# Delta rule of a fused two-block trunk: key products without masks, beta folded into VectorE's join, and turned keys ahead of the second query job

## The reference, cut to what matters

```python
gc = jnp.cumsum(chunks(g), axis=-1)
decay = jnp.exp(jnp.where(lower, gc[..., :, None] - gc[..., None, :], -jnp.inf))
k_beta = k * beta[..., None]
m = jnp.where(idx[:, None] > idx[None, :],
              jnp.einsum('bhnid,bhnjd->bhnij', k_beta, k) * decay, 0.0)
a_mat = eye + m
t_inv = lax.linalg.triangular_solve(a_mat, eye, left_side=True, lower=True, unit_diagonal=True)
...
intra = jnp.einsum('bhnid,bhnjd->bhnij', q, k) * decay
# scan over the chunks:
v_new = u_i - w_i @ s
o_i = (q_i * jnp.exp(g_i)[..., None]) @ s + a_i @ v_new
```

## Time and profile before

| | |
|---|---|
| median of three runs | 1927.75 us (1924.67 to 1928.99) |
| the profiled execution | 1928.05 us, its span 1926.2 us |
| busy: PE, DVE, ACT, POOL | 1820.8, 522.7, 429.1, 74.6 us |
| mean granted TensorE clock | 0.971 |
| input projection, convolutions and block inverses | about 52 to 228 us of the span |
| scan and modulation | about 228 to 294 us |
| experts | about 360 to 866 us |
| second block | from about 866 us on |

### The profile page before, as it was taken

The page is one execution under the profiler, slowest core; times in us unless marked ns, Lnnn a source line. Parts: engine busy times, 40 slices in busy tenths (PEclk is TensorE's granted clock), DMA queues, the critical chain, the costliest instruction groups (busy, mean ns, idle before and its releaser), DMA issues.

```text
span 1926.2 us, 25090 instructions
## 1 busy us (share of the span) xinstructions
PE 1820.8 (95%) x10394; PEld 1413.9 (73%) x10394; DVE 522.7 (27%) x1141; ACT 429.1 (22%) x925; POOL 74.6 (4%) x72
## 2 busy tenths in 40 slices
PE   6969898799999999999899999999999999899997
PEld 3665676566566666678678888888886688788886
DVE  3779441410000000022421212221234312212113
ACT  2542221111011110121542221111224522211112
POOL 0251000100000000010000100000000000000000
PEclk9889798899999999999999999999999999899999
DMA  9101178199999999973313324444443132234420
GB/s 394 42 22 66 54 276 333 77 398 422 422 422 422 422 422 422 422 305 138 130 66 132 109 110 150 152 151 152 140 137 131 47 128 110 88 134 152 155 84 22
DMA packets 53645, 383.32 MB, mean 199 GB/s; under 512 B 6208, under 2 KB 6336, under 8 KB 7360
## 3 DMA queue, kind: packets, MB, share of 16 engines
q1 hardware_dynamic: 52272, 376.97, 50.1%
q10 hardware_dynamic: 1296, 5.24, 0.7%
HBM read 381.14 MB, written 1.05 MB: 198 GB/s over the span
## 4 chain that ended last, share of the span: by engine, by line
PE 88%; DVE 8%; ACT 3%; issue 1%; DMA 1%; ACTq 0%; DVEq 0%
PE ps L575 84%; DVE arena L1962 3%; PE ps L573 2%; DVE ring L1956 1%; PE ps L632 1%; DVE arena L1956 1%; DVE arena L1959 1%; DMA ipos<-in_pos 1%; ACT arena L1720 1%; DVE small L2429 0%; DVE ring L2095 0%; DVE arena L2327 0%; ACT L1455 0%; DVE arena L1970 0%; ACT arena L1828 0%
## 5 line engine op out<-in xcount | busy, mean ns | idle before, releaser
L575 PE MATMUL ps<-arena,ring 128*128 128x256 f32 (+2 forms) x3680 | 832.5, 387 | 9.1 <-DVE arena L1962 3.9
L575 PEld LDWEIGHTS ps<-arena,ring 128*128 128x128 f32 x3680 | 694.8, 192 | 135.7 <-issue 42.4
L575 PE MATMUL ps<-ring,arena 128*64 128x256 f32 (+4 forms) x3168 | 484.2, 418 | 0.0
L575 PEld LDWEIGHTS ps<-ring,arena 128*64 128x64 f32 (+1 forms) x3168 | 292.9, 148 | 175.2 <-issue 87.2
L575 PE MATMUL ps<-arena 128*128 128x128 f32 (+5 forms) x1256 | 202.2, 322 | 6.6 <-DVE rounds_i L2283 1.8
L575 PEld LDWEIGHTS ps<-arena 128*128 128x128 f32 (+3 forms) x1256 | 166.8, 189 | 37.5 <-issue 22.8
L1962 DVE SCALAR_TENSOR_TENSOR arena<-ps,par,arena 128x255 f32<-128x255 f32 (+1 forms) x178 | 74.3, 480 | 336.5 <-ACT arena L1932 335.6
L575 PE MATMUL ps<-ring 128*128 128x256 f32 (+2 forms) x896 | 116.1, 301 | 8.9 <-DVE ring L2113 7.8
L575 PEld LDWEIGHTS ps<-ring 128*128 128x128 f32 (+2 forms) x896 | 98.5, 163 | 22.8 <-issue 10.1
L1932 ACT ACTIVATE arena<-ps,par 128x256 f32<-128x256 f32 x88 | 42.4, 562 | 313.6 <-PE ps L575 313.6
L575 PE MATMUL ps<-arena,cst 128*128 128x256 f32 (+1 forms) x308 | 91.2, 442 | 11.7 <-ACT arena L1748 5.4
(11 more groups left out here) (176 smaller groups left out, 852.0 us busy)
## 6 DMA issues: line engine op xcount, KB each, us to landing
ring<-in_stream SPq DMA_DIRECT2D x358, 1024.0 KB, 10.4
arena<-in_xc ACTq DMA_DIRECT2D x1, 1024.0 KB, 5.3
xT<-in_xc ACTq DMA_DIRECT2D x1, 1024.0 KB, 8.8
arena<-in_mem ACTq DMA_DIRECT2D x1, 1024.0 KB, 4.9
out_y<-xT ACTq DMA_DIRECT2D x2, 512.0 KB, 2.7
ring<-in_dft ACTq DMA_DIRECT2D x1, 512.0 KB, 8.0
arena<-in_sguw ACTq DMA_DIRECT2D x2, 256.0 KB, 2.9
par<-in_par SPq DMA_DIRECT2D x1, 511.5 KB, 24.6
```

The costliest lines, as they stand in the source:

```text
L575: i = nc.tensor.matmul(out, lhsT, rhs, start=start, stop=stop, skip_group_check=skip)
```

## The change

The strict triangle goes (both as a constant and as products): what lies above the diagonal of `bX` is no longer zeroed. Beta goes from GpSimd into the join on VectorE, as a per-partition scalar of a three-operand instruction, one for each head. All four `gQ` now come from ScalarE's second ReLU, get their exp there, and one mask product each on GpSimd; beta enters those of c = 4 and 6 at the later join on VectorE. The order of three engines is changed: TensorE turns the keys ahead of the job of the third query quarter; VectorE scales the keys after `conv(0)` and runs `conv(1)` to `conv(3)` behind that; ScalarE takes the root ahead of the third quarter's evacuation, and has the exponentials of `gQ` behind its copies of the keys.

```diff
@@ gpsimd
-            def mask(c):
-                s, d = c // 2, c % 2
-                v = bX[:, 4 * c:4 * c + 4, :]
-                pool.wait_ge(exp_ok2, c + 1)
-                link(tt(v, v, over(beta[:, d, (s, s ^ 1)[d], :], full_h, 2)))
-                if s >= 2 and d == 0:
-                    tt(gQ[:, c - 4], v, over(C("cum0"), full_h)).then_inc(gq_ok, 1)
-                tt(v, v, over(C("strict"), full_h)).then_inc(xm_ok, 1)
-            for c in range(4):
-                mask(c)
             pool.wait_ge(l2_ps, 1)
             link(nc.gpsimd.memset(bZ, 0.0))
             nc.gpsimd.memset(flatZ[:, 0:BLK * BLK:BLK + 1], 1.0).then_inc(fill_ok, 1)
-            for c in range(4, 8):
-                mask(c)
             pool.wait_ge(free, SLOTS)
             nc.gpsimd.memset(bB, 0.0)
             nc.gpsimd.memset(bF, 0.0).then_inc(fill_ok, 1)
-            for k, c in enumerate((5, 7)):
+            for k in range(4):
                 pool.wait_ge(exp_ok2, 9 + k)
-                tt(gQ[:, c - 4], gQ[:, c - 4], over(C("cum1"), full_h)).then_inc(gq_ok, 1)
+                tt(gQ[:, k], gQ[:, k], over(C(f"cum{k % 2}"), full_h)).then_inc(gq_ok, 1)
@@ tensor
             for c in range(6, 8):
                 rows(c)
-            s = arrive()
-            job_a(s, 0, hX, T)
-
             pe.wait_ge(l2_sq, 1)
...
             for t in range(4):
                 turns(KB[t], lambda hd: kT[:, hd, tok(t)], tr_k)
+            s = arrive()
+            job_a(s, 0, hX, T)
+
             job_a(s, 1, hX, T)
@@ scalar, falls(c): one ReLU per head more for c = 4 and 6
-                        if s >= 2:
-                            i = A_(gQ[:, c - 4, hd, :], ..., bias=gc[:, d, t, hd:hd + 1])
+                    if s >= 2:
+                        i = A_(gQ[:, c - 4, hd, :], ..., bias=gc[:, d, t, hd:hd + 1])
@@ scalar
             for c in range(4, 8):
                 decays(bX[:, 4 * c:4 * c + 4, :], c)
-            for c in (5, 7):
-                decays(gQ[:, c - 4], c)
-            evac_pad(2)
             act.wait_ge(l2_ps, 1)
             root(rk.rearrange("p t h -> p (t h)"), bank(5, 16), 1).then_inc(root_ok, 1)
+            evac_pad(2)
+            smooth(qT[:, 0, :])
             evac_pad(3)
+            evac_f(0)
             for t in range(4):
                 act.wait_ge(back_ps, t + 1)
                 A_(kT[:, :, t * P:t * P + P], bank((3, 4, 6, 7)[t], H1, P), ACT.Copy).then_inc(norm_ok, 1)
-            for j in range(4):
+            for c in range(4, 8):
+                decays(gQ[:, c - 4], c)
+            for j in range(1, 4):
                 smooth(qT[:, j, :])
                 evac_f(j)
@@ vector
             conv(7)
-            for j in range(4):
-                conv(j)
+            conv(0)
             rstd(rk)
             for t in range(4):
                 dve.wait_ge(tr_k, t + 1)
                 tt(ktok[:, t], bank(KB[t], H1, P), over(rk[:, t, :], full_h, 2)).then_inc(tok_ok, 1)
+            for j in range(1, 4):
+                conv(j)
             done = 0
-            for t in (0, 1, 2, 3):
+            for t in range(4):
                 dve.wait_ge(kk_ps, t + 1)
-                for c in sorted((2 * t, 2 * (t ^ 1) + 1)):
-                    dve.wait_ge(xm_ok, c + 1)
-                    v = bX[:, 4 * c:4 * c + 4, :]
-                    done = signal(tt(v, v, bank(KB[t], H1, P)), xk_ok, wait=False)
+                for s, d in ((t, 0), (t ^ 1, 1)):
+                    c = 2 * s + d
+                    dve.wait_ge(exp_ok2, c + 1)
+                    for hd in range(H1):
+                        v = bX[:, 4 * c + hd, :]
+                        i = stt(v, bank(KB[t], H1, P)[:, hd, :], beta[:, d, t, hd:hd + 1], v, MUL, MUL)
+                    done = signal(i, xk_ok, wait=False)
@@ vector, the join of gQ
                 for d in range(2):
                     k = 2 * (t ^ d) + d
-                    tt(gQ[:, k], gQ[:, k], bank(t, H1, P)).then_inc(aq_ok, 1)
+                    if d:
+                        tt(gQ[:, k], gQ[:, k], bank(t, H1, P)).then_inc(aq_ok, 1)
+                    else:
+                        for hd in range(H1):
+                            i = stt(gQ[:, k, hd, :], bank(t, H1, P)[:, hd, :], beta[:, 0, 2 + t, hd:hd + 1],
+                                    gQ[:, k, hd, :], MUL, MUL)
+                        i.then_inc(aq_ok, 1)
```

More of the change, by code:

```diff
@@ L73 @@
 ROW, N_ROW = offsets(ROW_1 + [(f"{n}{l}", k) for l in range(LAYERS) for n, k in ROW_L])
-CST, N_CST = offsets([("ident", P), ("ones", P), ("selv", 2), ("cum0", P), ("cum1", P), ("strict", P), ("dftc", 2 * P),
+CST, N_CST = offsets([("ident", P), ("ones", P), ("selv", 2), ("cum0", P), ("cum1", P), ("dftc", 2 * P),
                       ("invf", N_FREQ), ("first4", 4), ("first8", 8), ("iota", SLOTN)])
@@ L91, in constants @@
     put("cum1", j >= i)
-    put("strict", j < i)
     put("selv", j % 32 == np.arange(2)[None, :])
@@ L344, in trunk_kernel @@
         four_ps, four_g, four_cat = sem("four_ps"), sem("four_g"), sem("four_cat")
-        ha_ok, bd_ok, rows_ps, rel_ok, exp_ok2, xm_ok, gq_ok = [
-            sem("dec_" + n) for n in ("h", "bd", "rows", "rel", "exp", "x", "gq")]
+        ha_ok, bd_ok, rows_ps, rel_ok, exp_ok2, gq_ok = [
+            sem("dec_" + n) for n in ("h", "bd", "rows", "rel", "exp", "gq")]
         tr_k, tok_ok, back_ps, norm_ok, kk_ps, xk_ok = [
@@ L1525, in falls @@
                         i = A_(bX[:, 4 * c + hd, :], src[:, hd, :], ACT.Relu, bias=ngc[:, d, t, hd:hd + 1])
-                        if s >= 2:
-                            i = A_(gQ[:, c - 4, hd, :], src[:, hd, :], ACT.Relu, scale=-1.0,
-                                   bias=gc[:, d, t, hd:hd + 1])
+                    if s >= 2:
+                        i = A_(gQ[:, c - 4, hd, :], src[:, hd, :], ACT.Relu, scale=-1.0, bias=gc[:, d, t, hd:hd + 1])
                 i.then_inc(rel_ok, 1)
```

## The result

The changed kernel takes 1913.99 us (median of five, 1908.59 to 1914.34) against 1926.36 for the kernel before (median of five, 1922.06 to 1928.99): ratio 0.9932, 95% interval 0.9917 to 0.9946. That is 12.4 us by the medians, where 8.7 were forecast; timed again on another occasion it was 1915.31, ratio 0.9944 (0.9930 to 0.9957), 10.9 us. The profiled execution took 1914.24 us. A few executions took 1.2 to 3.3 times as long as the others; the ratios and their intervals leave them out, the medians in us do not. Kernels that were timed on different occasions are compared by their ratios to the kernel before.

The account below looks back on a forecast made before the run. The stretch before the inverse was taken as one chain with VectorE and TensorE each waiting for the other. Joins ending at 138.3 instead of 147.0 gave 8.7 us: 1928.05 - 8.7 = 1919.35, so 1919.1 us; range 1913.5 to 1925.

Parts of the forecast that it names:

- The path and its end at the inverse: New order walked through ScalarE, TensorE and VectorE: joins end at 138.3 us, inverse at 173.4, 8.7 us earlier.
- The sum: The 8.7 us gained at the inverse carried to the end: 1928.05 becomes 1919.35, hence 1919.1 us at the median.
- more gained: Rival: masks hold up nothing and TensorE's clock changes for the better, giving 1914 us; chance 0.08.
- the first place: TensorE's restart at 196.69 us behind the inverse, clock 0.50: one job took 6.25 us instead of 3.62; 2.6 could be saved.
- the idle time there: TensorE's wait for VectorE ahead of 196.69 us, 7.77 us; claimed to stay, as an argument against more being gained.
- Why the keys were late: Ahead of the scaled keys, GpSimd's two-operand products slow VectorE's convolution steps from 0.515 to 1.23 us.
- the masks' hold-ups: One GpSimd product holds up one VectorE convolution step for 0.71 us; four gQ masks cost 2.8 us.
- Half eaten: Rival: ScalarE's queue runs later or joins cost 0.40 us each, 4.2 us more, 1923 us; chance 0.14.
- nothing: Rival: TensorE decides instead of VectorE, or joins take 16.5 us, 1927 us; chance 0.08.
- slower: Rival: new 6 us wait ahead of the inverse keeps TensorE at 1.2 GHz up to the scan, 13 us, 1932; chance 0.04.
- the cover: Work right behind the inverse has 7.77 us of TensorE wait to hide a lower clock; argued against the slower rival.

Follow-up runs that it names:

- a kernel that ran with the changed one to within 0.3 us up to there: Changed kernel with the key products one projection job earlier on TensorE: 1916.15 us, ratio 0.9949 to the kernel before.
- three edits: Changed kernel plus gQ masks behind convolutions, root before exponentials, key products one job earlier: 1911.03 us, ratio 0.9919; same edits on new order with old arithmetic: 1913.24 us.
- order-only kernel: Three engines' order from the changed kernel, arithmetic from the kernel before: 1911.16 us, ratio 0.9918; timed again 1912.49 us, 0.9926.
- masks behind: Changed kernel with GpSimd's four gQ masks started only after the last q convolution: 1914.73 us, ratio 0.9955.
- wide joins: Changed kernel with eight joins of 128 x 512 in place of 32 of 128 x 128, leaving beta out of bX: 1911.93 us, ratio 0.9942.
- root first: Changed kernel with the root of the key norms ahead of bX's exponentials on ScalarE: 1911.11 us, ratio 0.9943.

## Why the prediction was right or wrong

**The path and its end at the inverse: right.** The joins ran from 129.44 to 137.8 us where 129.7 to 138.3 was forecast; counted from GpSimd's first product, they began at 63.2 and 62.7 where 62.5 was forecast. VectorE's reciprocal had its wait (9.83 for "9"), the masks cost 7.03 - 4.13 = 2.9 for 2.8, a join 8.36/32 = 0.26 for 0.27. The inverse came 9.0 us earlier for 8.7. The Trainium skill's fixed latency for each instruction ("VectorE: DVE Perf Modes", section on the errata) had put the 32 joins at an estimated 9.3 us; the measured 8.36 is below that, but the advice behind the rule holds: the wide ones are 3.5 us cheaper, shown by leaving beta out.

**The sum: mechanism right, size short.** The step that failed is the last one, in which the gain at the inverse was carried unchanged to the end. What lies behind it does not only move. Measured in the profiles, 9.0 us at the inverse became 10.4 at the norm and 13.9 at the end. The term left out is TensorE's clock. The first part (1.4) lies in the stretch behind the inverse, where the value job of the earlier trace rows took 5.68 us instead of 6.25, 0.57 of it; I did not single it out by an experiment. The second (3.3) lies in the last layer, more than 1.4 ms behind the change, and is shown to be the clock and not the change's own work: a kernel that ran with the changed one to within 0.3 us up to there lost it, its group of 16 matmuls taking 6.75 us instead of 5.15. Why the changed kernel kept it both times is open. I had set 0.08 on "more gained", named the first place, and said of the clock in general that the idle time there stays. The timed runs give 10.9 and 12.4 us by medians, between the 9.0 and the profiles' 13.9; how often the unprofiled executions take the short form of the last stage is open.

**Why the keys were late: the wrong cause stood first.** The prediction led with the masks' hold-ups. They exist at the price given (0.71 us each), but taking them away in the old order gave nothing (0.9994), and keeping them in the new order gave no less than the whole change (0.9918 and 0.9926 against 0.9944 and 0.9932; the intervals touch or overlap, and 10.4 against 9.0 us at the inverse is clear). The sum did not depend on the attribution, since it walked the new order through; a reader who had only that paragraph would have kept the wrong half. In the new order the new arithmetic costs 1.4 us at the inverse: the joins begin 2.1 us earlier, although ScalarE's root is 1.8 later, and last 3.5 longer.

**Two lines, nearly tied.** I had TensorE's first key product 2 us ahead of the joins. It was tied: counted from GpSimd's first product the products started at 62.1 us, not 59.5, mostly because the turned keys (3.64 us instead of 1.94) and the start of the query jobs behind them (8.07 us instead of 7.0) ran at 1.2 GHz. Nothing was lost by it here, but it is why three edits gave nothing alone and 3.0 us together. The wait ahead of the inverse was 3.66 us, not 6, for the same reason.

**Memsets were taken as free.** The earlier trace rows showed steps with two SBUF inputs running at full speed beside one, and I extended that to all. The one-input first step is held until the memset ends: 0.75 us here, 2.4 in the order-only kernel, 3.1 with the three edits. The Trainium skill ("SBUF — State Buffer", section "Who interferes with whom") says both: two SBUF inputs contend only with a GpSimd instruction that reads SBUF, and `tensor_scalar` in its 2-port mode with any. The traces agree (0.515 us a step beside the memset of the earlier trace rows, 2.73 for the other kind); I had used neither half.

**The rivals.** Half eaten, nothing and slower did not happen. TensorE did run at the lower clock behind the inverse (the first matmuls there took 3.62 us instead of 2.21), and the cover held, as argued.

## What to carry to other kernels

Walk the new order through engine by engine, with each queue's start and end; here it was right to 1 us at the place where the work meets again, while the obvious culprit (held-up steps) was worth nothing by itself. Before pricing an edit by itself, look how far behind the second line is: two lines within a microsecond of each other gave nothing to each of three edits alone and 3.0 us to all three together. When a saving is a few tenths of a per cent, compare profiles from an anchor that the change cannot reach, and expect some microseconds between that saving and the end from where the clock falls later on: in the twelve profiles of edited kernels here, 1.4 to 5.1 us more at the end than at the inverse. A microsecond that a profile shows at one place need not show in the timed runs.

## What the runs showed of the hardware that was not expected

Counted from a common instruction, executions of one kernel repeat to within 0.9 us over 1.85 ms (three kernels, two profiles each), the form of the last stage included, though the common instruction itself stands at 60.0 to 67.9 us of the span. And a stage that the change does not touch can last 9.0 or 10.4 to 10.6 us, and the one behind it 1.6 us less or more, with the granted clock. When it begins does not tell which: counted from the common instruction, the short form began at 1587.1 to 1591.1 us and the long one at 1590.49 too. The changed kernel, its repeat and the runs with masks behind, wide joins and root first have the short form, all others the long one. What decides between them was not found.
